# A hybrid state-space and attention backbone on one core: two gated halves split earlier in the last state-space step, a modulation turn moved behind the outputs, and two weight splits moved into the tile loops of two norms

## What is computed

```python
mod = (silu(c) @ w_mod[i] + b_mod[i]).reshape(-1, 6, 1024)      # shifts, scales, gates
hx  = modulate(rmsnorm(x, norm1_w[i]), mod[:, 0], mod[:, 1])
# mixer, layer 0: in projection, conv + silu, scan in 4 chunks of 128 tokens, both directions
y_intra = einsum('bijg,bijgr,bjgr,bjgrp->bigrp', cb, decay, dt_, x_)
y_state = einsum('bign,bgrpn->bigrp', c_, state) * exp(acum)[..., None]
out = gated_rmsnorm(y, z, norm_w) @ w_out                       # y * silu(z), 8 norm groups
x   = x + mod[:, 2][:, None] * out
hx  = modulate(rmsnorm(x, norm2_w[i]), mod[:, 3], mod[:, 4])
f   = (silu(h @ w1) * (h @ w3)) @ w2                            # dense; then the same with experts
```

## Time and profile before

| | |
|---|---|
| time, median of 3 | 2248.43 us |
| time of the profiled execution | 2248.92 us, its span 2246.8 us |
| PE busy | 2117.8 us, 94% of the span |
| DVE busy | 1465.2 us, 65% |
| ACT busy | 1231.6 us, 55% |
| chain that ended last | PE 82%, DVE 8%, ACT 4% |
| granted clock of TensorE, mean | 0.966 of 2.4 GHz |

### The profile page before, as it was taken

One profiled execution on the slowest core, in us unless ns is written; L12 is line 12 of the kernel. 1 busy time (PEld: TensorE's weight loads), 2 busy tenths in 40 slices (PEclk: granted clock), 3 DMA queues, 4 the chain that ended last, 5 costly groups with the idle time before them and its releaser, 6 DMA issues.

```text
span 2246.8 us, 26971 instructions
## 1 busy us (share of the span) xinstructions
PE 2117.8 (94%) x11268; PEld 1709.3 (76%) x11268; DVE 1465.2 (65%) x1389; ACT 1231.6 (55%) x1376; POOL 52.2 (2%) x20
## 2 busy tenths in 40 slices
PE   6889999979899999998887999999999999999997
PEld 4677878757677777887676788888888888888885
DVE  3567777763323332325546888888888988888885
ACT  4567666652322222215545766776766766776763
POOL 0011111100000000000000000000000000000000
PEclk9999999979899999998997999999999999999998
DMA  7233344432144444322305899899898999899891
GB/s 308 97 116 147 141 147 182 183 118 75 59 185 150 177 161 166 121 98 98 130 1 229 349 340 358 336 367 350 341 355 343 352 340 358 337 367 349 342 354 56
DMA packets 71777, 510.08 MB, mean 227 GB/s; under 512 B 7968, under 2 KB 8352, under 8 KB 10976
## 3 DMA queue, kind: packets, MB, share of 16 engines
q1 hardware_dynamic: 71568, 508.15, 59.7%
q10 hardware_dynamic: 80, 0.13, 0.0%
HBM read 504.97 MB, written 3.28 MB: 226 GB/s over the span
## 4 chain that ended last, share of the span: by engine, by line
PE 82%; DVE 8%; ACT 4%; issue 1%; DVEq 0%; ACTq 0%
PE ps L1087 14%; PE ps L1085 14%; PE ps L1086 14%; PE ps L659 10%; PE ps L661 10%; PE ps L660 10%; DVE area L1799 3%; DVE d_lo L1670 2%; ACT area L1324 1%; PE ps L1069 1%; PE ps L1116 1%; PE ps L671 1%; PE ps L756 1%; PE ps L1146 1%; ACT d_hi L1256 1%
## 5 line engine op out<-in xcount | busy, mean ns | idle before, releaser
L2118 DVE TENSOR_TENSOR w_lo<-w_raw,w_hi 128x2048 fp32r<-128x2048 f32 x336 | 748.5, 2287 | 59.1 <-ACT w_hi L1546 59.1
L1546 ACT ACTIVATE w_hi<-w_raw 128x2048 fp32r<-128x2048 f32 x336 | 625.3, 1919 | 77.0 <-PE ps L1087 75.7
L1670 DVE TENSOR_TENSOR d_lo<-d_raw,d_hi 128x2048 fp32r<-128x2048 f32 (+1 forms) x76 | 171.9, 2262 | 329.8 <-ACT d_hi L1256 329.8
L1085 PE MATMUL ps<-w_hi,x_hi 128*128 128x512 f32 x896 | 358.1, 400 | 5.1 <-DVE x_lo L2173 5.1
L1087 PE MATMUL ps<-w_hi,x_lo 128*128 128x512 f32 x896 | 356.0, 397 | 0.0
L659 PE MATMUL ps<-h_top,d_hi 128*128 128x512 f32 (+1 forms) x816 | 331.3, 406 | 25.2 <-DVE h_low L1662 9.8
L1086 PE MATMUL ps<-w_lo,x_hi 128*128 128x512 f32 x896 | 351.6, 392 | 0.0
L1256 ACT ACTIVATE d_hi<-d_raw 128x2048 fp32r<-128x2048 f32 (+1 forms) x76 | 143.8, 1891 | 373.1 <-DMA d_raw<-in_dense 235.7
L661 PE MATMUL ps<-h_top,d_lo 128*128 128x512 f32 (+1 forms) x816 | 322.8, 396 | 0.0
L660 PE MATMUL ps<-h_low,d_hi 128*128 128x512 f32 (+1 forms) x816 | 318.9, 391 | 0.0
L659 PEld LDWEIGHTS ps<-h_top,d_hi 128*128 128x128 f32 x816 | 158.3, 194 | 69.6 <-issue 26.2
(11 more groups left out here) (289 smaller groups left out, 2487.9 us busy)
## 6 DMA issues: line engine op xcount, KB each, us to landing
w_raw<-in_experts SPq DMA_DIRECT2D x336, 1024.0 KB, 4.8
d_raw<-in_dense SPq DMA_DIRECT2D x120, 1024.0 KB, 5.3
area<-acum_rows SPq DMA_DIRECT2D x16, 1024.0 KB, 7.6
d_raw<-in_dense SPq DMA_DIRECT2D x4, 768.0 KB, 4.3
xT<-in_xt SPq DMA_DIRECT2D x4, 512.0 KB, 6.4
gate_rows<-area SPq DMA_DIRECT2D x4, 512.0 KB, 6.8
hT<-gate_rows SPq DMA_DIRECT2D x2, 1024.0 KB, 6.2
cst<-in_consts SPq DMA_DIRECT2D x2, 512.0 KB, 12.1
```

The lines of the kernel that those rows point to most:

```text
L1085: mm(o, hi, w_hi[u % HIGH][:, a:a + 512], start=first, stop=False)
L1546: A(w_hi[n % HIGH][:], w_raw[n % RAW][:], ACT.Copy).then_inc(S["whi_done"], 1)
L1670: TT(d_lo[u][:, 0:w], d_raw[u][:, 0:w], d_hi[si % D_HIGH][:, 0:w].bitcast(F32), ALU.subtract)\
L2118: TT(w_lo[n % RAW][:], w_raw[n % RAW][:], w_hi[n % HIGH][:].bitcast(F32), ALU.subtract)\
```

## The change

```diff
 # PE, last group
             mod_pair(11, 5)
             pe.wait_ge(S["st_op"], 80)
-            turn_pair(11, 4)
             out_part(1, 0, range(8)).then_inc(S["d_used"], 1)
             outputs(7)
+            turn_pair(11, 4)
             out_part(0, 1, range(8, 14))
 # ACT, last group
             gate_high(0)
+            gate_high(1)
             segments(7)
             token_evac(7)
-            gate_high(1)
+            dense_high(W0 + 1)
             row_exps(7)
-            dense_high(W0 + 1)
 # ACT, norms
-            def split_tiles(j, l, shift):
+            def split_tiles(j, l, shift, si):
                 for k in range(KT + 1):
                     ...
+                    if k == 3:
+                        dense_high(si)
-            dense_high(W0 + 9)
             root(1)
-            split_tiles(1, 0, 3)
+            split_tiles(1, 0, 3, W0 + 9)
-            dense_high(W0 + 43)
             root(2)
-            split_tiles(2, 1, 0)
+            split_tiles(2, 1, 0, W0 + 43)
 # DVE, last group
             finish(6)
+            gate_low(1)
             token_scales(7)
             merge(7)
-            gate_low(1)
+            dense_low(W0 + 1)
+            state_ops(7)
             carried(7)
             decayed(7)
-            dense_low(W0 + 1)
-            state_ops(7)
             skip(7)
             mod_rows(11)
-            mod_out(11)
             gate_low(2)
             dense_low(W0 + 2)
             gated(7)
+            mod_out(11)
 # DVE, norms
+            norm_split(1)
             dense_low(W0 + 9)
-            norm_split(1)
 ...
+            norm_split(2)
             dense_low(W0 + 43)
-            norm_split(2)
```

## The result

The changed kernel takes 2235.11 us (median of 6 runs, 2234.05 to 2238.08) against 2248.22 us for the kernel before on the same occasions: the ratio is 0.9943, with a 95% interval of 0.993 to 0.9956. That is 13.1 us less; 14.4 were forecast. It was measured again beside the last experiments at 2233.9 us, ratio 0.9934 (0.9921 to 0.9948). The profiled execution took 2235.25 us, its span is 2233.2 us.

The account below looks back on a forecast made before the run. PE was taken to bound the kernel, busy 94% of the span, so only its waits count. Gains of 10.3 (last group), 3.8 and 0.4 us (norms) sum to 14.5 off 2248.92, giving a predicted median of 2234.0 us, range 2230.5 to 2238.5.

Parts of the forecast that it names:

- Chunk 1: Last group: ACT runs chunk 1 ahead of the exponentials once its transfer lands at 461.3; PE's 7.75 us wait goes.
- The new stop: Last group: PE still waits 3.5 us, now for the state operations, which run from 481.7 to 485.6.
- Slow work behind the stop: Last group: the clock falls after PE's stop for the state operations, costing 2.4 us, bounds 0 and 2.9.
- Turn and slack: Last group: the moved turn takes 0.9 us, decayed(7) is ready 8 us early for the outputs; group gain 10.3 us.
- Norm 1: First norm: spread 3.1 us earlier, 1.0 from full clock, less 0.3 for the copy; gain 3.8 us.
- the term for the full clock: First norm: the spread runs at full clock in half its time, gaining 1.0 us, bounds 0 and 1.0.
- Norm 2: Norm ahead of attention: spread gains 2.5 and 1.0 us; copy 1.9, new wait 1.0, clock 0.2 leave 0.4 us.
- the page's drain: Second norm: by the skill page a table switch adds about 1380 ns of drain, making the norm -1.0 us.
- the clock that stays up: Rival, last group: no slow work after the new stop, 2.4 us more gain, 2231.6 us; chance 0.15.
- The late transfer: Rival, last group: transfers into hT land late, at 472 say, leaving about 2243 us; chance 0.05.
- the norms give nothing: Rival, both norms: spreads stay slow, PE pays the copy in the first too; gain 10.9 or 10.4, 2238; chance 0.16.
- The slow clock that decides the sign: Rival, after the new stop: PE stays at the lower clock; slower from 16.9 us of such work, up to 2266; chance 0.02.

Follow-up runs that it names:

- norms_only: The changed kernel with the last state-space group as before, so only the weight splits in the two norms are moved; 2245.2 us, ratio 0.9984.
- turn_undone: The changed kernel with the modulation turn back ahead of the second out projection unit and its DVE half back behind mod_rows; 2242.78 us.
- states_undone: The changed kernel with carried and decayed back ahead of the weight rest and state operations, and ACT's weight split back behind the row exponentials; 2239.95 us.
- filler: The changed kernel with eight idle matmuls in PE's stop ahead of the second out projection unit; 2234.29 us, ratio 0.9936.
- run both: The changed kernel with the states ahead of the first out projection's last two k tiles and the second norm's weight split ahead of its last two squares; 2233.46 us.
- chunk_undone: The changed kernel with chunk 1 of the gated halves back behind the copies on ACT and behind merge on DVE; 2242.48 us.
- states_early: The changed kernel with the last two k tiles of the first out projection unit moved behind the states; 2232.94 us, ratio 0.9931.
- filled: The kernel of run both plus idle matmuls in five of PE's stops, at the mixer's last k tiles and around both norms' spreads; 2227.58 us, ratio 0.9909.

## Why the prediction was right

The forecast was 2234.0 us and 14.5 us off the profiled execution; the spans differ by 13.6. By its steps:

- **Chunk 1.** Forecast: the transfer has landed at 461.3, everything behind the exponentials 2.1 us later, PE without a wait. Measured: 461.11 with a wait of 0.29 us, `token_scales` at 474.79 (474.95 forecast), no wait of PE. Right.
- **The new stop.** Forecast 3.5 us, until 485.6; measured 2.15 us, until 486.50. The term that was off is the start and pace of `out_part(0, 0)`: I took the first half from the trace before and 0.238 us for each matmul of the second, but the clock was low when they began. `to_tokens` ahead of them (L748) took 2.08 us here and in nine other profiles, and 1.16 in before, norms_only, turn_undone and states_undone. So the states began at 479.90 instead of 477.6. That used up part of the stop ahead of it; and the state operations, which the forecast had waiting for nothing from PE, waited 0.97 us for the states and began at 482.53 instead of 481.7, so the stop ended later. Where L748 was fast the step came out as forecast: in turn_undone the state operations began at 481.46 and PE had been ready since 482.0. The place was right and its size was not; which of the two cases an execution falls into was not foreseen.
- **Slow work behind the stop.** Forecast 2.4 us, with 4 to 6 us of slow work; the run filler measures it as 44.92 - 43.36 = 1.6 us, and about 3.4 us were slow.
- **Turn and slack.** The turn took 0.98 us (0.9 forecast), the outputs waited for nothing. The group gives 10.0 us where 10.3 were forecast: the stop ended 0.9 us too late and the slow work cost 0.8 us less, so the two errors above cancel. That the outputs began at 499.49, where 499.4 was forecast, is luck in this part.
- **Norm 1.** The spread starts 3.1 us sooner, as forecast, but the clock was not at its full level during it: it took 1.65 us where about 1 was forecast, and the mean granted clock from 582.85 to 584.50 was 0.65. From its start to the first tile are 588.79 - 582.85 = 5.94 us instead of 602.85 - 596.21 = 6.64: 0.7 us, where the term for the full clock was 1.0. From the first tile to the modulation product behind the unit are 602.55 - 588.79 = 13.76 us instead of 616.16 - 602.85 = 13.31 (the row of the chain in the earlier trace rows has 616.23 for the same product): the copy in the tile loop costs 0.45 us (0.3 forecast). Together 3.3, also by the stretches, instead of 3.8.
- **Norm 2.** The spread starts 2.3 us sooner (2.5 forecast), and took 1.16 us (1.04 forecast). Then come the stops of 1.66 and 1.11 us (1.9 and 1.0 forecast). The first tile starts 3.24 us sooner behind the first sums (3.5 forecast), and from it to the first rotation are 1026.74 - 1007.36 = 19.38 us instead of 1040.43 - 1024.20 = 16.23, so 3.15 us are given back (3.1 forecast). Together 0.1 instead of 0.4. The root again began with the end of the table load (999.22 + 1.28 = 1000.50, root at 1000.51), so nothing like a drain is seen here either. By the figure of the Trainium skill, page "ScalarE: Activation LUTs", section "What ACT_TABLE_LOAD costs", the spread would have gained about 1.1 us (an estimate, the forecast's 2.5 less the 1.4 of the page's drain); the measured 2.3 speak against it.

The rivals: the clock that stays up did not come about (0.64 in the 4.5 us behind the stop, where run filler had 1.00). The late transfer did not either. That the norms give nothing did not come: together they give 3.4. The second gives 0.1, but not as this rival had it, by a slow spread; the spread was fast, and the copy and the new wait took back what it gained, as in the forecast's own sum. The slow spreads that the rival names were seen in run both. The slow clock that decides the sign was not seen; after the stop about 3.4 us were slow. The upper end of the range was set a little low: the worst case took 2.0 us for norm 1, where the rival's own terms leave 3.8 - 1.0 - 1.6 = 1.2, which gives about 2239.

What stays open: which edit would shorten the time ahead of the last group, and what sets where in it the clock is low; no kernel here changed it.

## What to carry to other kernels

When an operation is moved out of a chain, ask of the new place what paces it: the copy that hid in a norm where PE was behind its tiles (0.4 us) cost all it had gained in one where PE waited for each tile. A better place was ahead of the last two squares, where ACT had stood idle for 7.33 us: there the copy delayed the spread by 0.7 us and gave 1.9 us in all. What is lost when one edit is undone is not its share of the whole, since the stop that comes back takes up what the others save: here 6.8, 7.6 and 5.6 us undone one by one stand against 10.0 together. For effects of a few us, compare stretches between two fixed instructions of the profile. In the two profiles of one kernel they repeated to 0.05 us where the whole time scattered by 4. But kernels with the same code in a stretch can differ there: norm 2 to the router took 179.38 us in chunk_undone and 181.30 in states_undone. So a gain counts only in the stretch that the edit touches, and below 2 us it wants more than one profile.

## What the runs showed of the hardware

- The granted clock can fall behind a stop of 2.15 us (0.64 over the next 4.5 us), and the work behind it then loses 1.6 us. Behind a stop of 2.39 us at one and the same instruction it was 1.00 over 5.2 us in the changed kernel, 0.67 in filler, which had come to it 1.6 us sooner, and 1.00 in states_early, which had come to it 2.9 us sooner. Whether a given stop costs something is no property of the stop alone. With the five further stops filled the mean granted clock was 0.974 against 0.970 for run both, the same kernel with its stops open, and the span was 6.3 us lower; 3.3 of these are the different start described next.
- The time ahead of the last group lay between 452.75 and 456.25 us in fourteen profiles of kernels that agree up to there. Two executions side by side show two places where they part, the first sums (L615) and the first turn (L643). PE's timeline at the start of run filler:

```profile
8.19 1.08 PE L615 MATMUL ps<-area,cst 128*32 128x128 f32 x16 [8.19 <-ACT area L1208]
...
19.52 1.05 PE L643 MATMUL ps<-cst 128*128 128x2 f32 x8 [0.82 <-DVE cst L1704]
```

And of run both:

```profile
9.60 3.58 PE L615 MATMUL ps<-area,cst 128*32 128x128 f32 x48 [9.60 <-ACT area L1206]
...
21.03 1.86 PE L643 MATMUL ps<-cst 128*128 128x2 f32 x8 [0.81 <-DVE cst L1704]
```

The first sums came 1.4 us later, and the first turn ran at about half the pace, 1.86 against 1.05 us; by the last group the difference is 3.5 us. These two places don't explain all of it: chunk_undone, states_undone and filled had the slow first turn too (1.87 us) and came to the last group at 453.28, 452.95 and 453.00. What else differs in between was not followed.
